# Hybrid decoder layer on one core: key pages three a slot and value pages four a slot, the latter from eight buffers and none beside the output projection

## The reference

```python
k_past = cache_k[l, page_table].reshape(db, past, N_HEADS, HEAD_DIM)
v_past = cache_v[l, page_table].reshape(db, past, N_HEADS, HEAD_DIM)
...
s = jnp.einsum('bqhd,bkhd->bhqk', q, k, preferred_element_type=jnp.float32) * (HEAD_DIM ** -0.5)
s = s + jnp.transpose(c_q, (0, 2, 1))[:, :, :, None] - jnp.transpose(c_k, (0, 2, 1))[:, :, None, :]
p = jax.nn.softmax(s, axis=-1)
return jnp.einsum('bhqk,bkhd->bqhd', p.astype(v.dtype), v)
```

## Time and profile before

| | |
|---|---|
| median of 3 runs | 2901.93 us (2901.82 to 2904.88) |
| the profiled execution | 2906.3 us, span 2904.4 us |
| PE busy | 2654.7 us, 91% |
| DVE busy | 1428.7 us, 49% |
| ACT busy | 730.8 us, 25% |
| moved by DMA | 532.92 MB, mean 183 GB/s |

### The profile page before, as it was taken

One profiled execution on the slowest core, in us unless ns is written; L12 is line 12 of the kernel. 1 busy time (PEld: TensorE's weight loads), 2 busy tenths in 40 slices (PEclk: granted clock), 3 DMA queues, 4 the chain that ended last, 5 costly groups with the idle time before them and its releaser, 6 DMA issues.

```text
span 2904.4 us, 50517 instructions
## 1 busy us (share of the span) xinstructions
PE 2654.7 (91%) x19656; PEld 2329.5 (80%) x19656; DVE 1428.7 (49%) x5629; ACT 730.8 (25%) x979; POOL 156.2 (5%) x317
## 2 busy tenths in 40 slices
PE   5899899963767779998999999999999999999998
PEld 3799889851323226666999999999999999999998
DVE  4786677669776142224343434344443434343433
ACT  4332122212223241123222122222222222222221
POOL 0100000001111221200000000000000000000000
PEclk8999999986766989998999999999999999999999
DMA  6789899887999867735223322222322222332221
GB/s 237 250 285 336 311 334 349 305 303 281 356 369 371 288 208 276 267 130 179 88 90 105 98 88 88 88 88 95 105 92 88 88 88 88 99 105 88 88 88 63
DMA packets 274530, 532.92 MB, mean 183 GB/s; under 512 B 16410, under 2 KB 177787, under 8 KB 272980
## 3 DMA queue, kind: packets, MB, share of 16 engines
q1 hardware_dynamic: 214573, 361.52, 36.3%
q0 software_dynamic: 39472, 142.46, 13.5%
q10 hardware_dynamic: 20247, 25.73, 2.5%
HBM read 503.94 MB, written 24.05 MB: 182 GB/s over the span
## 4 chain that ended last, share of the span: by engine, by line
PE 77%; DMA 10%; DVE 8%; issue 2%; SPq 1%; ACT 1%; POOLq 0%; ACTq 0%; POOL 0%; DVEq 0%
PE ps L678 76%; DMA t_r<-in_cache_k 6%; DVE t_work L1746 5%; DMA t_r<-in_cache_v 2%; DMA t_wraw<-in_w_in 1%; PE ps L681 1%; DVE t_wl L1583 0%; SPq L563 0%; ACT t_wh L1196 0%; DMA t_auxW<-in_pool_w 0%; DVE t_work L1583 0%; DVE t_xl L1583 0%; DVE t_auxW L1583 0%; DMA t_wraw<-in_w_o 0%; SPq L549 0%
## 5 line engine op out<-in xcount | busy, mean ns | idle before, releaser
L678 PE MATMUL ps<-t_xh,t_wh 128*128 128x260 f32 (+1 forms) x4352 | 951.6, 294 | 19.3 <-DVE t_xl L1583 19.2
L678 PE MATMUL ps<-t_xh,t_wl 128*128 128x260 f32 (+1 forms) x4352 | 937.8, 291 | 0.0
L678 PE MATMUL ps<-t_xl,t_wh 128*128 128x260 f32 (+1 forms) x4352 | 936.6, 291 | 0.0
L1583 DVE TENSOR_TENSOR t_wl<-t_wraw,t_wh 128x1024 fp32r<-128x1024 f32 x376 | 460.0, 1224 | 897.9 <-ACT t_wh L1196 897.9
L1196 ACT ACTIVATE t_wh<-t_wraw 128x1024 fp32r<-128x1024 f32 x376 | 398.0, 1060 | 1657.9 <-PE ps L678 1657.9
L678 PEld LDWEIGHTS ps<-t_xh,t_wh 128*128 128x128 f32 x4352 | 687.8, 190 | 99.4 <-issue 65.5
L678 PEld LDWEIGHTS ps<-t_xh,t_wl 128*128 128x128 f32 x4352 | 687.8, 190 | 11.9
L678 PEld LDWEIGHTS ps<-t_xl,t_wh 128*128 128x128 f32 x4352 | 687.6, 190 | 9.1
L1746 DVE CUSTOM_DVE_ANT_0 t_work<-t_r,t_work 128x128 f32<-128x128 f32 x2048 | 454.6, 285 | 130.8 <-DMA t_r<-in_cache_k 118.9
L678 PE MATMUL ps<-t_hh,t_wh 128*128 128x260 f32 x1408 | 285.2, 284 | 3.4 <-issue 3.4
L678 PE MATMUL ps<-t_hh,t_wl 128*128 128x260 f32 x1408 | 284.3, 283 | 0.0
(11 more groups left out here) (256 smaller groups left out, 1202.4 us busy)
## 6 DMA issues: line engine op xcount, KB each, us to landing
t_r<-in_cache_k SPq DMA_DIRECT2D x256, 512.0 KB, 6.9
t_r<-in_cache_v POOLq DMA_DIRECT2D x256, 512.0 KB, 6.1
t_wraw<-in_w_up SPq DMA_DIRECT2D x44, 2048.0 KB, 8.0
t_wraw<-in_w_in SPq DMA_DIRECT2D x22, 2048.0 KB, 9.4
t_wraw<-in_w_down SPq DMA_DIRECT2D x22, 2048.0 KB, 7.8
t_wraw<-in_w_o SPq DMA_DIRECT2D x11, 2048.0 KB, 10.2
scr_proj<-t_stg ACTq DMA_DIRECT2D x40, 256.0 KB, 4.4
t_aux<-scr_proj ACTq DMA_DIRECT2D x8, 768.0 KB, 12.3
```

The lines of the kernel that those rows point to most:

```text
L678: return pe.matmul(out, lhsT, rhs, start=start, stop=stop)
L1583: return dve.tensor_tensor(out, in0, in1, op)
```

## The change

`page_slots` puts three key pages in each slot from 2 to 89 (two at a sequence's start), and value pages from slot 81: two a slot up to slot 92, four a slot in slots 93 to 150, none after. `LAST` becomes 150, so the join of the samples' attention moves from slot 176 to slot 152, the first output chunk. While no keys are left and the residual isn't loaded yet (value pages in slots 90 to 148), the key ring serves as four more value buffers: pages whose number modulo 8 is 4 to 7 are loaded into it by SP, 116 in all; POOL loads the other 140. The residual's load waits for the last of those pages, 247.

```diff
-K_RATE = 2
 def page_slots():
     keys, values, k_end, v_end = {}, {}, [], []
-    for n in range(DEC * PAGES):
-        keys.setdefault(KEY0 + n // K_RATE, []).append(n)
-    for r in range(DEC):
-        k_end.append(KEY0 + (PAGES * (r + 1) - 1) // K_RATE)
-    at = 0
+    at, n = KEY0, 0
+    while n < DEC * PAGES:
+        take = 3 if n % PAGES else 2
+        keys[at] = list(range(n, n + take))
+        k_end += [at] * ((n + take) // PAGES - n // PAGES)
+        n += take
+        at += 1
+    at = CHUNKS + 1
     for r in range(DEC):
         at = max(at, k_end[r] + 4)
         done = 0
         while done < PAGES:
-            rate = ((2 if at % 2 == 0 else 0) if at < CHUNKS else (2 if at % 3 else 0) if at < k_end[-1] else
-                    (4 if at % 2 == 0 else 2))
+            rate = 2 if at < HEAD0 else 4
...
+def value_places():
+    slot_of = {n: s for s, pages in VALUES.items() for n in pages}
+    places, held, loads = [], {}, [0] * RING + [DEC * PAGES // RING] * RING
+    for n in range(DEC * PAGES):
+        b = n % (2 * RING if K_END[-1] < slot_of[n] < TAIL else RING)
+        loads[b] += 1
+        places.append((b, loads[b], held.get(b, -1)))
+        held[b] = n
+    return places, max(held.get(b, -1) for b in range(RING, 2 * RING)), loads
...
             def value_loads(pages):
+                pages = [n for n in pages if V_PLACES[n][0] < RING]
...
-                    pool.wait_ge(v_used, n + 1)
-                    pool.dma_start(vring[:, n % RING, :],
+                    b, _, held = V_PLACES[n]
+                    pool.wait_ge(v_used, held + 1 + PRIME)
+                    pool.dma_start(vring[:, b, :],
...
                 if s == TAIL:
                     sp.wait_ge(k_used, DEC * PAGES + PRIME)
+                    sp.wait_ge(v_used, V_WIDE + 1 + PRIME)
...
+                vp = [n for n in VALUES.get(s, []) if V_PLACES[n][0] >= RING]
+                vg = [number(n) for n in vp]
+                for n, g in zip(vp, vg):
+                    b, _, held = V_PLACES[n]
+                    if held < 0:
+                        sp.wait_ge(k_used, DEC * PAGES + PRIME)
+                    else:
+                        sp.wait_ge(v_used, held + 1 + PRIME)
+                    sp.dma_start(kring[:, b - RING, :],
+                                 v_pages[bass.ds(g, 1), :, :].rearrange("a p n -> (a p) n")).then_inc(k_loaded[b - RING], 16)
...
             def value_page(r, p):
-                pe.wait_ge(v_loaded[p % RING], r * (16 * PAGES // RING) + 16 * (p // RING + 1))
+                b, load, _ = V_PLACES[r * PAGES + p]
+                pe.wait_ge((v_loaded + k_loaded)[b], 16 * load)
+                buf = vring[:, b, :] if b < RING else kring[:, b - RING, :]
```

More of the change, by code:

```diff
@@ L86 @@
 assert LAST + 4 < SLOTS
+def value_places():
[7 more added lines that the diff above has]
+    return places, max(held.get(b, -1) for b in range(RING, 2 * RING)), loads
+V_PLACES, V_WIDE, V_LOADS = value_places()
 K_LAST = {s: r for r, s in enumerate(K_END)}
@@ L480, in value_loads @@
             def value_loads(pages):
+                pages = [n for n in pages if V_PLACES[n][0] < RING]
                 numbers = [pool.value_load(ptr[0:1, n:n + 1], min_val=0, max_val=N_POOL - 1) for n in pages]
                 for n, g in zip(pages, numbers):
-                    pool.wait_ge(v_used, n + 1)
-                    pool.dma_start(vring[:, n % RING, :],
-                                   v_pages[bass.ds(g, 1), :, :].rearrange("a p n -> (a p) n")).then_inc(v_loaded[n % RING], 16)
+                    b, _, held = V_PLACES[n]
+                    pool.wait_ge(v_used, held + 1 + PRIME)
+                    pool.dma_start(vring[:, b, :],
+                                   v_pages[bass.ds(g, 1), :, :].rearrange("a p n -> (a p) n")).then_inc(v_loaded[b], 16)
             for s in range(SLOTS):
@@ L820, in value_page @@
             def value_page(r, p):
-                pe.wait_ge(v_loaded[p % RING], r * (16 * PAGES // RING) + 16 * (p // RING + 1))
+                b, load, _ = V_PLACES[r * PAGES + p]
+                pe.wait_ge((v_loaded + k_loaded)[b], 16 * load)
+                buf = vring[:, b, :] if b < RING else kring[:, b - RING, :]
                 for c in range(2):
                     lane = 32 * (2 * (p % 2) + c)
-                    last = mm(ps[lane:lane + HEADS, 4, :], Eb[:, r * PAGES + p, :], vring[:, p % RING, c * 512:(c + 1) * 512],
+                    last = mm(ps[lane:lane + HEADS, 4, :], Eb[:, r * PAGES + p, :], buf[:, c * 512:(c + 1) * 512],
                               p < 2, p >= PAGES - 2)
@@ L1086, in between @@
                         for i in range(RING):
-                            pe.wait_ge(v_loaded[i], 16 * (DEC * PAGES // RING + 1))
+                            pe.wait_ge(v_loaded[i], 16 * (V_LOADS[i] + 1))
                         sample_out_attention(10, lambda k, c: vring[:, 2 * k + c // 2, 512 * (c % 2):512 * (c % 2 + 1)])\
```

## The result

| | before | after |
|---|---|---|
| median | 2903.4 us (2901.8 to 2905.2, 4 runs) | 3010.9 us (3003.1 to 3017.6, 4 runs) |
| span of the profiled execution | 2904.4 us | 3015.8 us |

The ratio is 1.0369 (95% interval 1.0342 to 1.0397): slower, as forecast, but by 108 us where 45 were forecast, and above the range of 2885 to 2993.

The account below looks back on a forecast made before the run. The prediction took DVE's key pages to bound projection and mixers, and DMA the heads. First stretch +54, heads +30, tail +10, output projection -49 gave +45 on 2901.9: 2947 us, range 2885 to 2993.

Parts of the forecast that it names:

- DVE's work: Projection and mixers: DVE needs 603 us for key pages, softmax and its other work, where the stretch took 618.
- The waits for keys: Projection: key pages behind weight loads in SP's queue stall DVE 3.3 us a load, 17 loads, 56 us.
- The bytes of the heads: Heads: 224 value pages and 3.7 MB of residual make 131.6 MB, where the stretch carried 112.25 MB before.
- the price of 0.66 us a page in the output projection: Output projection: 7.9 us for 12 value pages, 0.66 each; 62 pages removed from chunks 2 to 22 save 41 us.
- the wait behind the first chunk: Tail: PE's wait for the samples' attention sums, 5.76 us before, now comes right behind the first output chunk.
- tail and output together: Tail, 1050 to 1090 us, +10 (between 5 and 18); output projection without value pages, -49.
- two signs named for being wrong: The prediction is wrong if the first head starts before some 740 us or the heads take clearly less than 350.
- Sum: 603 + 69 = 672: Projection and mixers: 603 us of DVE work plus 69 of stalls and small terms, against 618: +54.
- the wait for the mixers' loads: Mixers: this wait after the last chunk falls away, as PE finishes the projection some four slots ahead of DVE.
- At the 364 GB/s that a share of 0.98 gave, 361.5 us: Heads: DMA binds, 131.6 MB at 364 GB/s take 361.5 us, +30; bounds 355 us (+23) and 385 us (+53).
- The eight buffers: Rival, heads: eight buffers bring no gain, pages keep 2.14 us each, 480 us; 3065 us in all, chance 0.04.
- PE at a low clock: Rival, heads: PE binds at clock 0.70, 7.1 us a slot, 400 us, 38 more; 2985 us in all, chance 0.12.

Follow-up runs that it names:

- e4: The kernel after, with value page loads (but the first into each buffer) cut to 64 of 1024 columns, matmuls kept: 2901.6 us.
- f1: The kernel after, with the heads' value pages in one ring of four buffers, all loaded by GpSimd: 3092.7 us.
- f3: The kernel after, with three value pages a slot beside the heads and 61 pages beside the output projection: 2964.7 us.
- k3: The kernel after, with weight loads on ScalarE's queue, three value pages a slot beside the heads and 61 beside the output projection: 2920.5 us.

## Why the prediction was wrong in size and right in direction

**Right.** DVE's work: 603 us forecast, 500.94 + 90.91 in the two windows and 599.6 up to the first head. The waits for keys: 56 forecast behind the weight loads, 66.6 - 9.7 at the start = 57 measured, a few of them not behind a load. The bytes of the heads, the price of 0.66 us a page in the output projection, the wait behind the first chunk, tail and output together -43 against -39. Neither of the two signs named for being wrong came: the first head was at 811.5 us, not before 740, and the heads didn't take less than 350. Both looked for an error on the cheap side only.

**The first stretch, "Sum: 603 + 69 = 672".** DVE stood for 112 us, not 69. Of the 43 us too little, some 22 are gaps of under 0.5 us between instructions, 18 of them between a page and the next, which I had costed at nothing by adding busy times (1.785 a page). A page with its gap, 1.785 + 0.144 = 1.93, on the slot of 4.77 gives the 6.70 measured. Some 14 lie in the mixers, where I had 4: 8.0 for key pages, 6.2 for PE and 3.4 for ScalarE, 17.6 in all. For the 6.2 the sentence that failed is that the wait for the mixers' loads falls away "since PE finishes the projection some four slots ahead of DVE". PE can't: each sequence's end binds it to DVE's `t_mx` (93.7 us of waits), the last one in the projection from 687.5 to 693.4, so it was about one slot ahead, and it stood 13.55 us for that load. Another 6.4 is the wait for weight heads. The busy part was 3 us too high.

**The heads, "At the 364 GB/s that a share of 0.98 gave, 361.5 us".** I took the rate of the 212 us in which two engines, DVE and PE, each emptied a ring of their own. After, PE alone empties both rings, between the heads' own steps, at a clock of 0.77. The share fell to 0.88 and the rate to 328 GB/s, where the lower end of my range was 0.92 and 342; 390.4 us lies above its 385. e4 (276 us without the bytes) and f1 (464 with half the buffers) show that PE's work alone isn't the limit, and the 12 us in which PE was busy throughout at a clock of 0.50 and the DMA engines stood at 0.51 show that the transfers alone aren't either. No run held the clock up with the bytes in place, so what the clock costs by itself stays open. The stretch before, taken whole, had said it: 112.25 MB in 332 us are 338 GB/s, and 131.6 MB at that rate take 389 us, +57. That this comes out within 2 us is in part luck, since the two stretches differ in what they hold. The price of a page moved out of the heads, 1.4 to 1.7 us in f3 and k3, is near the 1.44 that the prediction had by the bytes; what it had wrong is that the whole stretch would run at the best rate.

**The rivals.** The eight buffers do something: f1. PE at a low clock, 2985 us: the clock was indeed low, 0.77 on the mean, and my argument that it "cannot last" failed: PE was busy for 0.83 of the 402 us, and the clock stood between 0.66 and 0.86 in every window of 50 us. But PE without the wait for bytes takes 276 us, so it isn't that alone, and 2985 was still below the result. The range's upper end, 2993, already held the upper ends of three terms at once (23 us for the heads, 15 for the loads, 8 for the tail). It was passed because the gaps (22 us), the weight heads (6) and most of the mixers' waits (14) had no term and no range, and because the heads passed their own upper end by 7.

## What to carry to other kernels

Where work moves from one engine's bound to another's, add up slots as the timeline spaces them, with their gaps, and not busy times alone; and look for the points at which the leading engine must wait for the new slow one, since they cap its lead. The best transfer rate of a stretch with two consumers need not hold where a single one empties the buffers between other work, at a clock that falls when it waits: here 364 GB/s became 328. Take the mean of the whole stretch as one of the bounds. A busy share of 0.955 on the bounding engine still hid 6% of a stretch (517 us against 484): moving the big loads out of the small pages' queue gave 31 us to the kernel before, more than any placement of pages tried on it.

## What the runs showed of the hardware that I had not expected

A longer landing of the 512 KB pages went with a higher rate: 4.9 us and 291 GB/s with four buffers, 7.6 to 7.9 and 328 with eight. A page that stood behind a 2 MB load in the same queue landed 12.3 us after the load's issue; with the loads on another queue DVE's longest wait for a page from 100 us on was 2.1 us, while a load itself took 17.1 in place of 11.0. And a value page that PE had waited for took it 1.88 us at a granted clock of 0.50 and 1.03 at 1.00.
